# Gated linear attention state updates: contraction over 32 rows with two masked key copies, in place of 128 rows with eight

## The reference

```python
def step(S, blk):
    qc, kc, vc, bc = blk                     # one block of C = 16 tokens
    tot = bc[:, :, -1:, :]
    q_dec = qc * jnp.exp(bc)
    k_dec = kc * jnp.exp(-bc)
    k_end = kc * jnp.exp(tot - bc)
    A = jnp.where(causal, jnp.einsum('bhtk,bhsk->bhts', q_dec, k_dec), 0.0)
    o = jnp.einsum('bhtk,bhkv->bhtv', q_dec, S) + jnp.einsum('bhts,bhsv->bhtv', A, vc)
    S = S * jnp.exp(tot)[:, :, 0, :, None] + jnp.einsum('bhsk,bhsv->bhkv', k_end, vc)
    return S, o
```

## Time and profile before

| | us |
|---|---|
| median of 3 runs | 1347.73 |
| lowest, highest | 1338.66, 1350.14 |
| profiled execution | 1347.76 |
| its span, first to last instruction | 1345.9 |
| PE busy in the span | 1270.2 (94%) |
| DVE, POOL, ACT busy | 773.2, 435.9, 344.2 |
| mean granted PE clock | 0.946 |

### The profile page before, as it was taken

One profiled execution on the slowest core, in us unless ns is written; L12 is line 12 of the kernel. 1 busy time (PEld: TensorE's weight loads), 2 busy tenths in 40 slices (PEclk: granted clock), 3 DMA queues, 4 the chain that ended last, 5 costly groups with the idle time before them and its releaser, 6 DMA issues.

```text
span 1345.9 us, 23075 instructions
## 1 busy us (share of the span) xinstructions
PE 1270.2 (94%) x8883; PEld 1186.6 (88%) x8883; DVE 773.2 (57%) x1238; ACT 344.2 (26%) x536; POOL 435.9 (32%) x203
## 2 busy tenths in 40 slices
PE   5899999999999978999989997979999999999995
PEld 4899999999999966999966554969999999999995
DVE  4988988888662276688546866683323323322114
ACT  3322212211111143432223444133122122211111
POOL 0244433443344322333231100323334333433432
PEclk9699999999999988899959995989999999999998
DMA  9244444444442323121200010111222222222232
GB/s 378 91 168 163 164 162 158 170 165 139 141 142 83 90 82 146 46 80 64 85 1 1 1 40 1 63 63 63 86 86 78 78 88 84 74 75 82 82 83 82
DMA packets 39664, 132.08 MB, mean 98 GB/s; under 512 B 4720, under 2 KB 5888, under 8 KB 38720
## 3 DMA queue, kind: packets, MB, share of 16 engines
q1 hardware_dynamic: 39616, 131.43, 29.4%
HBM read 128.05 MB, written 3.36 MB: 98 GB/s over the span
## 4 chain that ended last, share of the span: by engine, by line
PE 77%; issue 14%; DVE 4%; POOL 3%; ACT 1%; DMA 1%; DVEq 0%; POOLq 0%; SPq 0%; ACTq 0%
PE acc L704 63%; PE acc L722 3%; POOL w_lo L379 3%; PE aux L1017 2%; PE aux L893 2%; PE aux L1001 2%; PE acc L924 2%; PE aux L981 1%; DMA x<-x_in 1%; PE aux L776 1%; DVE rstd L1079 1%; PE acc L968 1%; DVE h_lo L1095 0%; PE acc L905 0%; DVE y L1471 0%
## 5 line engine op out<-in xcount | busy, mean ns | idle before, releaser
L379 POOL TENSOR_TENSOR w_lo<-raw,w_hi 128x1024 fp32r<-128x1024 f32 (+2 forms) x182 | 410.2, 2254 | 815.2 <-ACT w_hi L458 815.2
L458 ACT ACTIVATE w_hi<-raw 128x1024 fp32r<-128x1024 f32 (+2 forms) x182 | 175.7, 966 | 806.6 <-PE acc L704 769.6
L704 PE MATMUL acc<-h_hi,w_hi 128*128 128x288 f32 x1760 | 378.9, 297 | 1.6 <-POOL w_lo L379 1.6
L704 PE MATMUL acc<-h_lo,w_hi 128*128 128x288 f32 x1760 | 378.3, 297 | 0.0
L704 PE MATMUL acc<-h_hi,w_lo 128*128 128x288 f32 x1760 | 378.2, 297 | 0.0
L704 PEld LDWEIGHTS acc<-h_hi,w_hi 128*128 128x128 f32 x1760 | 284.6, 189 | 4.4 <-issue 2.6
L704 PEld LDWEIGHTS acc<-h_hi,w_lo 128*128 128x128 f32 x1760 | 285.0, 190 | 0.0
L704 PEld LDWEIGHTS acc<-h_lo,w_hi 128*128 128x128 f32 x1760 | 284.9, 189 | 0.0
L1116 DVE CUSTOM_DVE_ANT_0 aux<-ada,cond_all 128x1024 f32<-128x1024 f32 x112 | 186.2, 1663 | 19.6 <-DMA ada<-w_ada_rows_in 16.5
L1161 DVE TENSOR_TENSOR tmp_a<-tmp_a,acc 128x576 f32<-128x576 f32 x44 | 33.2, 754 | 208.7 <-PE acc L704 202.7
L704 PE MATMUL acc<-g_lo,w_hi 128*128 128x288 f32 x704 | 150.8, 296 | 0.0
(11 more groups left out here) (170 smaller groups left out, 1082.4 us busy)
## 6 DMA issues: line engine op xcount, KB each, us to landing
ada<-w_ada_rows_in SPq DMA_DIRECT2D x56, 512.0 KB, 3.3
raw<-w_gate_in SPq DMA_DIRECT2D x44, 512.0 KB, 3.4
raw<-w_up_in SPq DMA_DIRECT2D x44, 512.0 KB, 3.2
raw<-w_down_in SPq DMA_DIRECT2D x32, 384.0 KB, 3.1
raw<-w_in_in SPq DMA_DIRECT2D x22, 512.0 KB, 3.2
raw<-w_down_in SPq DMA_DIRECT2D x32, 320.0 KB, 2.9
ada_rows<-w_ada_rows_in SPq DMA_DIRECT2D x4, 1024.0 KB, 16.9
ada_units<-w_ada_units_in SPq DMA_DIRECT2D x4, 1024.0 KB, 19.6
```

The source lines that it names most:

```text
L379: pool.tensor_tensor(w_lo[:, slot, 0:nk, :], raw[:, slot, 0:nk, :], w_hi[:, slot, 0:nk, :].bitcast(F32), ALU.subtract).then_inc(split, 1)
L458: act.activation(w_hi[:, slot, 0:nk, :], raw[:, slot, 0:nk, :], ACT.Copy).then_inc(rounded, 1)
L704: ins = pe.matmul(acc[:, 2 * b + half, 0:HALF], w[:, slot, n, :], a[:, k, HALF * half:HALF * (half + 1)], start=first and n == 0 and m == ...
```

## The change

`k_block` becomes two copies for each tile, even blocks and odd blocks, in two buffers by tile; POOL makes both with one instruction of 128x512 elements for a tile. The mask has two columns, `parity`. `addition` takes the 32 rows that hold blocks b and b + 1 (b even), and the copy in which the other block of the pair is zero. Waits follow: one `block_ready` for a tile, and POOL waits for the additions of the tile two back, where it had waited for those of the tile before.

```diff
-for _name, _width in (("ident", P), ("causal", P), ("block", 8), ("carry", T), ("dist", 512), ("qk_sum", 50),
+for _name, _width in (("ident", P), ("causal", P), ("parity", 2), ("carry", T), ("dist", 512), ("qk_sum", 50),
...
-        k_block = place("k_block", [P, 8, 2 * P])
+        k_block = place("k_block", [P, 2, 2, 2 * P])
...
             for i, (t0, nt, _, _) in enumerate(TILES):
-                for half in range(nt // (4 * GBLOCK)):
-                    blocks = slice(4 * half, 4 * half + 4)
-                    pool.wait_ge(tok_ready, i + 1)
-                    if i:
-                        pool.wait_ge(u_made, 8 * i - 4 + 4 * half)
-                    pool.tensor_tensor(
-                        k_block[0:nt, blocks, :],
-                        k_tok[0:nt, :].rearrange("p (o n) -> p o n", o=1).to_broadcast([nt, 4, 2 * P]),
-                        c("block", nt)[:, blocks].rearrange("p (n o) -> p n o", o=1).to_broadcast([nt, 4, 2 * P]),
-                        ALU.mult).then_inc(block_ready, 1)
-                    if i == 0 and half == 0:
-
-                        pool.wait_ge(block_ready, 1)
...
+                pool.wait_ge(tok_ready, i + 1)
+                if i >= 2:
+                    pool.wait_ge(u_made, 8 * (i - 1))
+                pool.tensor_tensor(
+                    k_block[0:nt, i % 2, :, :],
+                    k_tok[0:nt, :].rearrange("p (o n) -> p o n", o=1).to_broadcast([nt, 2, 2 * P]),
+                    c("parity", nt).rearrange("p (n o) -> p n o", o=1).to_broadcast([nt, 2, 2 * P]),
+                    ALU.mult).then_inc(block_ready, 1)
+                if i == 0:
+
+                    pool.wait_ge(block_ready, 1)
...
                 if i:
-                    act.wait_ge(block_ready, 2 * i)
+                    act.wait_ge(block_ready, i)
...
-                pe.wait_ge(block_ready, 2 * i + b // 4 + 1)
+                pe.wait_ge(block_ready, i + 1)
                 if n:
                     pe.wait_ge(s_ready, n)
                 for h in range(GLA_HEADS):
                     rows = slice(GLA_DK * (h % 2), GLA_DK * (h % 2) + GLA_DK)
-                    ins = pe.matmul(aux[rows, 3, P * (h // 2):P * (h // 2) + P], k_block[0:nt, b, GLA_DK * h:GLA_DK * (h + 1)],
-                                    v_tok[0:nt, i % 2, P * h:P * h + P], start=True, stop=True)
+                    tokens = slice(2 * GBLOCK * (b // 2), 2 * GBLOCK * (b // 2 + 1))
+                    ins = pe.matmul(aux[rows, 3, P * (h // 2):P * (h // 2) + P],
+                                    k_block[tokens, i % 2, b % 2, GLA_DK * h:GLA_DK * (h + 1)],
+                                    v_tok[tokens, i % 2, P * h:P * h + P], start=True, stop=True)
                 ins.then_inc(u_made, 1)
...
-    put("block", p[:, None] // GBLOCK == np.arange(8)[None, :])
+    put("parity", p[:, None] // GBLOCK % 2 == np.arange(2)[None, :])
```

More of the change, by code:

```diff
@@ L413, in _ @@
             for i, (t0, nt, _, _) in enumerate(TILES):
-                for half in range(nt // (4 * GBLOCK)):
-                    blocks = slice(4 * half, 4 * half + 4)
-                    pool.wait_ge(tok_ready, i + 1)
-                    if i:
-                        pool.wait_ge(u_made, 8 * i - 4 + 4 * half)
-                    pool.tensor_tensor(
-                        k_block[0:nt, blocks, :],
-                        k_tok[0:nt, :].rearrange("p (o n) -> p o n", o=1).to_broadcast([nt, 4, 2 * P]),
-                        c("block", nt)[:, blocks].rearrange("p (n o) -> p n o", o=1).to_broadcast([nt, 4, 2 * P]),
-                        ALU.mult).then_inc(block_ready, 1)
-                    if i == 0 and half == 0:
-                        pool.wait_ge(block_ready, 1)
[L427 to L432, removed]
+                pool.wait_ge(tok_ready, i + 1)
[8 more added lines that the diff above has]
+                    pool.wait_ge(block_ready, 1)
+                    for r in range(2):
+                        if r:
+                            pool.wait_ge(q_zero, 1)
+                        rows = slice(GLA_DK * (1 - r), GLA_DK * (2 - r))
+                        pool.memset(q_half[rows, :, r, :], 0.0).then_inc(q_zero, 1)
+                    pool.wait_ge(q_zero, 2)
             paired(WOUT + 2, KD)
```

## The result

| | before | after |
|---|---|---|
| median, us | 1348.93 (4 runs) | 1379.04 (4 runs) |
| lowest, highest | 1338.66, 1350.25 | 1370.9, 1382.36 |
| profiled execution, its span | 1347.76, 1345.9 | 1382.36, 1380.4 |
| PE busy | 1270.2 | 1307.4 |
| POOL busy | 435.9 | 423.8 |

What follows compares the result with a forecast made beforehand. PE (TensorE), busy 94% of the span, was taken as the bound, its clock unsettled in this stretch. 1347.76 - 0.95 + 0.8 = 1347.6, plus 25.2 and 10.5 for the clock, gave 1383.3, rounded 1384; range 1346 to 1400 us.

Steps and rivals of the forecast that it cites:

- rival A: Rows do not count for the PE clock, so the sum is 1347.6 us, within 1%; chance 0.26.
- (1): POOL's k_block multiply: half the elements, 0.95 us in place of 1.90 for the first one on the path; saves 0.95 us.
- (2): Waits of POOL, PE and ACT are met earlier or at the same time as now: cost and gain 0.
- (3): GLA addition matmuls contract over 32 rows but keep 0.59 us a step at the full clock: cost 0.
- (4): Six additions following L1001 blocks no longer run beside them: 0.11 us lost each, 0.2 at slow clock; 0.8 us taken.
- (5): From 709 us in the GLA stage, additions with fewer rows in use lose the full clock: 25.2 + 10.5 us; chance 0.67.
- First term: Return of the full clock moves from 709 to 746 us: 33.6 us x 0.75 = 25.2 us.
- Second term: Two clock falls after 746 us, ahead of the L1001 blocks behind slots 20 and 28: 14 x 0.75 = 10.5 us.
- B: Full clock returns long before 709 us: 13 us less, 1334; chance 0.04 for a gain of over 1%.
- C: All 36 GLA steps pay two borders for the 32-row form, 0.1 us each: 7.2 us, 1355, within 1%; chance 0.03.

Runs made afterwards that it cites:

- the two row experiments: Additions over all rows in the changed kernel: 1345.53 us, ratio 0.996; additions over 32 rows in the kernel before, eight copies kept: 1383.46 us, ratio 1.0252.
- The run with all rows again: Changed kernel with the addition contracting over all rows of the tile again, everything else of the change kept: 1345.53 us, ratio 0.996.
- the fillers' profile: Kernel before plus five unread matmuls of 128 rows and 512 columns in PE's waits between 672 and 679 us; profiled execution; ratio of the runs 0.9981.
- the narrow fillers: Kernel before plus five unread matmuls at the stage's start, contracting over 32 rows instead of 128: median 1347.25 us, ratio 0.9999.
- End fillers: Seven more unread matmuls in PE's waits from slot 36 on, added to the kernel before with five start fillers and 128-row spreads: 1342.44 us, ratio 0.9947.

## Why the prediction was right

The forecast was 1384 with 1346 to 1400; measured were 1379.04, and 1382.36 for the profiled execution. The range is so wide that it holds rival A's 1347.6 as well, so the time inside it says little; the clock rows and the two row experiments carry the case. Step by step:

**(1) The multiply.** 1.05 us in place of 1.90, where 0.95 was estimated. The saving on the path is 0.85 and not 0.95. Small, and drowned by the rest.

**(2) The waits.** The run with all rows again carries all of the changed waits and times as before. Cost 0 holds within its interval.

**(3) Rows do not set an instruction's time.** 0.58 and 1.05 us for 32 rows; 0.59 (0.58 over 64 rows) and 1.05 before. Right.

**(4) The six borders.** The addition no longer runs beside L1001. At the slow clock, two L1001 records and the addition take 1.90 + 1.05 = 2.95 us in the chain of the changed kernel (from 704.80). In the chain of the kernel before the same place reads:

```profile
706.19 0.42 PE aux L1001
706.61 0.21 PE aux L893
706.82 0.20 issue
707.03 1.06 PE aux L1001
708.09 0.85 PE aux L893 x6
708.94 0.28 PE aux L981
```

from 706.19 to 708.94, 2.75 us. The loss is 0.20 at the slow clock, as forecast; six of them, if alike, make about 1 us. The rule of the Trainium skill, "TensorEngine Tiling (Array Packing)", section Tiling Modes, that a change of mode drains the engine, fits; no run here separates the drain from the lost company.

**(5) The clock.** The mechanism was right in its main point: with fewer rows in the additions and PE as busy, the stage loses the full clock. Its two terms were both mis-sized, and the errors cancelled.

- First term, 25.2 us for a return handed on from slot 4's block to slot 16's. It came behind slot 12's, at 746.5 (743.34 and 746.80 in the chain above). That the forecast said 746 too is chance: its 746 was a time of the kernel before, at which slot 16 ends. Slot 12 ended at 732.8 there and at 746.5 here, so that the term measured 13.7 us, with some 1 us of the borders in it and the earlier start taken off.
- Second term, 10.5 us for two falls. There were three, 750.0, 777.3 and 787.5, holding 44.3 us of slow clock: 44.3 x (1 - 1/1.77) = 19.3 us. Only the fall at 777.3 came where the forecast had one, ahead of slot 20's block; the one ahead of slot 28's did not come. Those at 750.0 and 787.5 had not been foreseen; each came some 3.5 us behind a return.
- Together 13.7 + 19.3 = 33.0, against 35.7 forecast.

The chain, read from block to block, needs no factor. Slot 12's block ends at 746.80 here and 733.26 before, 13.5 us later. From there to the end of slot 28's it is 77.8 us here (to 824.62) and 56.8 before (to 790.06), so that the further falls cost 21.0, twice what was forecast for them. The two make the 34.5 us by which the span grew. The row of before:

```profile
733.26 0.44 PE aux L893 x6
```

**The rivals.** A (rows do not count) fell by both row experiments. It stood on the section The HAM clock gate of "TensorE: Matmul & The Clock Gate" in the Trainium skill, where busy time alone is named; here PE is busy 69.35 of 71.60 us at the slow clock, and the measurement decides. B (an early return by the change) did not come; that PE does more in those 29 us at the full clock is shown by the fillers' profile (212 records against 142 in the slow one of the narrow fillers), what it is worth in the time is not. C (every border of the 32-row form costs) fell: steps away from L1001 keep their 0.58 us.

What was only argued: why the clock came back behind slot 12 and not slot 8 or 16, and why one kernel's executions fall into groups some 8 us apart. Nor is it shown that the count of rows is what matters: each edit of the rows also changed where the additions can run side by side with L1001 (both 32 and 64 rows stand alone). That 64 rows cost 1.2% and 32 cost 2.5%, with the same company lost, and that L968 sorts by its rows too, speak for the count. The profiled executions show different places of the clock's changes; no run here sets them.

## What to carry to other kernels

A matmul over fewer rows cost the same time here (0.58 us a step over 32 rows, 0.59 over 128); in a stretch of small matmuls whose clock is unsettled, it can take the full clock away from everything around it. Before cutting contraction rows (or masks, or padding) as waste, read the granted clock of the stretch in windows, and where it is unsettled, keep the rows or even pad them with zero weights. Wide matmuls whose results nobody reads, where PE waits at the start of such a stretch, paid here only together with padded spreads (0.9908 and 0.9899); neither alone was told from no change. Look at many executions: one profile shows one of several courses.

## What had not been expected

- Padding a 4-row and a 10-row contraction to 128 rows with zero weights did not lengthen them (2.10 us for the eight records of L854 in place of 2.20, both at the full clock).
- 64 rows brought the full clock back no earlier than 32 did (747.8 and 748.4), and one execution with 128 rows was as late (749.5).
- End fillers left the slow clock at the stage's end as long as it was, 20.5 us.
- A kernel whose clock is unsettled has a spread of its own: 30 runs of the kernel before lay between 1337.37 and 1353.66 us, 1.2%, seven of them below 1340 and none from there to 1343.8. The kernel with start fillers fell into two groups as well, around 1338 and 1346. A change of under 1% can't be read from a few runs here.
